# Moving the fading of layer 1's states from VectorE to GpSimd

## The reference

```
cb = einsum('bign,bjgn->bijg', C, B)
y  = einsum('bijg,bijgr,bjgrp->bigrp', cb, lmat * dt, x)
y  = y + einsum('bign,bgrpn->bigrp', C, S) * exp(acum)        # the part from the state
w  = exp(a_last - acum) * dt
S  = exp(a_last) * S + einsum('bjgn,bjgr,bjgrp->bgrpn', B, w, x)   # faded, then added to
```

## Time and profile before

| | us |
|---|---|
| median of 3 runs | 1554.14 |
| range of the runs | 1553.2 to 1556.65 |
| the profiled execution | 1551.42 |
| its span, first to last instruction | 1549.7 |

### The profile page before, as it was taken

How to read it: one execution, slowest core, us unless ns; L and a number is a source line. 1 busy time by engine, 2 the same in 40 slices (tenths; PEclk the granted TensorE clock), 3 DMA queues, 4 the chain that set the end, 5 groups by cost and what they waited for, 6 DMA issues and landing times. The chain is left out here.

```text
span 1549.7 us, 31393 instructions
## 1 busy us (share of the span) xinstructions
PE 1447.2 (93%) x11610; PEld 1195.0 (77%) x11610; DVE 1175.9 (76%) x2595; ACT 822.4 (53%) x1837; POOL 248.7 (16%) x438
## 2 busy tenths in 40 slices
PE   6999999799999979899999999989999999999985
PEld 5979787666788858898888888767787777777754
DVE  4555587856786887968977898986879787587775
ACT  4735353446465544546655765653657364655451
POOL 5010113101231200012111112120003110000012
PEclk8999999999999999999999999999999999999998
DMA  6455455335476542547854764843585664554541
GB/s 190 132 155 148 129 168 151 112 114 171 120 205 191 160 122 71 150 122 182 253 145 121 237 191 140 240 140 94 167 247 143 189 183 144 175 150 150 175 137 61
DMA packets 283778, 243.11 MB, mean 157 GB/s; under 512 B 32856, under 2 KB 251036, under 8 KB 283468
## 3 DMA queue, kind: packets, MB, share of 16 engines
q1 hardware_dynamic: 273708, 208.28, 45.6%
q0 software_dynamic: 9920, 32.84, 7.9%
HBM read 180.40 MB, written 64.97 MB: 158 GB/s over the span
## 5 line engine op out<-in xcount | busy, mean ns | idle before, releaser
L1447 PE MATMUL bank<-h,w 128*128 128x268 f32 (+1 forms) x4752 | 835.3, 330 | 22.5 <-ACT w L857 15.8
L1447 PEld LDWEIGHTS bank<-h,w 128*128 128x128 f32 x4752 | 699.4, 191 | 102.1 <-issue 28.4
L873 DVE TENSOR_TENSOR w<-w_raw,w 128x1024 fp32r<-128x1024 f32 x132 | 160.9, 1219 | 35.5 <-ACT w L857 34.9
L842 PE MATMUL bank<-s_w_out,s_yt_hi 128*128 128x512 f32 (+2 forms) x544 | 169.8, 402 | 3.8 <-DVE s_ys L2532 3.8
L857 ACT ACTIVATE w<-w_raw 128x1024 fp32r<-128x1024 f32 x132 | 138.7, 1051 | 8.1 <-DMA w_raw<-in_ssd_w_in_dram 8.1
L1525 DVE SCALAR_TENSOR_TENSOR conv<-before_conv,cw,conv 128x260 f32<-128x260 f32 (+2 forms) x216 | 125.3, 580 | 4.2
L842 PEld LDWEIGHTS bank<-s_w_out,s_yt_hi 128*128 128x128 f32 (+2 forms) x544 | 97.1, 182 | 30.8 <-issue 4.4
L842 PE MATMUL bank<-g_w_out,g_ot_hi 128*128 128x512 f32 (+2 forms) x288 | 97.0, 426 | 1.6 <-DVE g_ot_lo L2073 1.3
L842 PE MATMUL bank<-s_w_out,s_yt_lo 128*128 128x512 f32 x240 | 95.6, 398 | 0.0
L2616 ACT ACTIVATE s_yt_hi<-bank 128x512 fp32r<-128x512 f32 (+1 forms) x36 | 20.1, 557 | 126.5 <-PE bank L2607 126.4
L2319 ACT ACTIVATE s_decay<-s_decay,t_ac 128x128 f32<-128x128 f32 (+1 forms) x288 | 85.4, 379 | 1.2
(11 more groups left out here) (256 smaller groups left out, 2503.4 us busy)
## 6 DMA issues: line engine op xcount, KB each, us to landing
w_raw<-in_ssd_w_in_dram SPq DMA_DIRECT2D x80, 512.0 KB, 4.3
w_raw<-in_gla_w_in_dram SPq DMA_DIRECT2D x48, 512.0 KB, 4.3
s_decay<-kept_acd SPq DMA_DIRECT2D x32, 512.0 KB, 6.2
w_raw<-in_ssd_w_out_dram SPq DMA_DIRECT2D x30, 512.0 KB, 4.0
g_chunk<-kept_gq SPq DMA_DIRECT2D x32, 448.0 KB, 4.9
s_chunk<-kept_sq SPq DMA_DIRECT2D x32, 384.0 KB, 4.8
kept_sq<-stage SPq DMA_DIRECT2D x80, 134.0 KB, 4.3
kept_sq<-stage SPq DMA_DIRECT2D x40, 256.0 KB, 4.7
```

What stands on the lines that cost most here:

```text
L842: last = pe.matmul(bank[0:r, :], yt[a][:, k, 0:r], wo[:, b, 512 * half:512 * half + 512], start=(k + a + b == 0), stop=(k == tiles - 1 and ...
L873: dve.tensor_tensor(self.part(i, 1), self.raw(i), hi, ALU.subtract).then_inc(self.w_lo, 1)
L1447: last = pe.matmul(bank[:, 0:n], w[:, p.tile % 2, a, k, :], h[:, b, k, c:c + n], start=(i == 0), stop=(i == len(terms) - 1))
```

## The change

GpSimd does the fade of the state, in a new function pool_fade, called at each scan with s > 0 at the scan's place in the list. It waits for the decay (el_done) and for TensorE's read of the old state (inter). VectorE scales the state part first, after a wait for s_prod, then waits for the new semaphore s_faded and adds SU. The semaphore aexped is given up for the new one: the exponential of a_log now counts on exped.

```diff
@@ program, gpsimd
             elif name == "keep":
                 ssd.pool_keep(pool, *at)
+            elif name == "scan" and at[2]:
+                ssd.pool_fade(pool, *at[1:])
@@ Sizes.act_log
         if G == 0:
-            act.activation(self.m["aexp"][:, :], self.m["alog"][:, :], ACT.Exp).then_inc(self.aexped, 1)
+            act.activation(self.m["aexp"][:, :], self.m["alog"][:, :], ACT.Exp).then_inc(self.exped, 1)
         act.wait_ge(self.absd, GROUP_CGS[G][-1] + 1)
         act.activation(t1, t1, ACT.Exp, scale=-1.0).then_inc(self.exped, 1)
-        act.wait_ge(self.exped, G + 1)
+        act.wait_ge(self.exped, G + 2)
@@ Sizes.dve_sum
-        dve.wait_ge(self.aexped, 1)
@@ Ssd.dve_scan
-        dve.wait_ge(self.el_done, e + 1)
         if s:
+            dve.wait_ge(self.el_done, e + 1)
             dve.wait_ge(self.inter, self.z_count(u, s) + 1)
-            kept = self.mark(dve.tensor_tensor(heads(S), heads(S), self.by_head(t["el"][:, e % 2, :], P), ALU.mult))
             dve.wait_ge(self.s_prod, e + 1)
-            dve.wait_ge(self.chain, kept)
+            from_state = self.mark(dve.tensor_tensor(heads(xw[0:n, :]), heads(self.Y[1][0:n, :]),
+                                                     self.by_head(t["ea"][0:n, e % 2, :], n), ALU.mult))
+            dve.wait_ge(self.s_faded, self.z_count(u, s) + 1)
             dve.tensor_tensor(S, S, self.SU[:, :], ALU.add).then_inc(self.s_new, 1)
         if not self.last_unit(u, s):
             skip()
-        if s:
-            from_state = self.mark(dve.tensor_tensor(heads(xw[0:n, :]), heads(self.Y[1][0:n, :]),
-                                                     self.by_head(t["ea"][0:n, e % 2, :], n), ALU.mult))
         dve.wait_ge(self.intra, e + 1)
         dve.wait_ge(self.skipped, e + 1)
@@ Ssd
+    def pool_fade(self, pool, u, s):
+
+        e, q, heads = ev(u, s), self.z_count(u, s), self.split_heads
+        S = self.S[:, u % 2, :]
+        pool.wait_ge(self.el_done, e + 1)
+        pool.wait_ge(self.inter, q + 1)
+        pool.tensor_tensor(heads(S), heads(S), self.by_head(self.t["el"][:, e % 2, :], P),
+                           ALU.mult).then_inc(self.s_faded, 1)
```

More of the change, by code:

```diff
@@ L1174, in __init__ @@
         self.m, self.d = m, d
-        (self.small_in, self.aexped, self.absd, self.exped, self.logged, self.dt_done, self.a_done, self.scanned, self.ea_done, self.stored) = (
-             sem("size_" + x) for x in ("small_in", "aexped", "absd", "exped", "logged", "dt_done",
+        (self.small_in, self.absd, self.exped, self.logged, self.dt_done, self.a_done, self.scanned, self.ea_done, self.stored) = (
+             sem("size_" + x) for x in ("small_in", "absd", "exped", "logged", "dt_done",
                                         "a_done", "scanned", "ea_done", "stored"))
@@ L2174, in __init__ @@
          self.yt_lo, self.out_done, self.added, self.xdc_ready, self.spread, self.answered, self.ss_kept, self.ss_new, self.s_turned, self.s_kept, self.parked, self.s_saved,
-         self.z0_in, self.z0_turned, self.answers_turned) = (
+         self.z0_in, self.z0_turned, self.answers_turned, self.s_faded) = (
              sem("s_" + x) for x in (
@@ L2180, in __init__ @@
                  "xdc_ready", "spread", "answered", "ss_kept", "ss_new", "s_turned",
-                 "s_kept", "parked", "s_saved", "z0_in", "z0_turned", "answers_turned"))
+                 "s_kept", "parked", "s_saved", "z0_in", "z0_turned", "answers_turned", "s_faded"))
     def mark(self, ins):
```

## The result

| | before | changed |
|---|---|---|
| median of the runs, us | 1553.67 | 1573.05 |
| range of 4 runs each, us | 1552.95 to 1556.65 | 1570.38 to 1574.33 |
| the profiled execution, us | 1551.42 | 1573.76 |
| its span, us | 1549.7 | 1572.1 |

The changed kernel is slower: its time is 1.0116 times that of before, with a 95% interval of 1.0101 to 1.0131, some 19 us. The forecast was +8, with a range that ended at 1567. The sign was right, the size was not.

A forecast was written before the change was run, and what follows sets the result against it. TensorE, busy 93%, was taken as the bound, with time lost only where it stands still. Middle part +4.75 and last unit +3.05 gave +7.8 us, 1562 on the median; forecast's own range 1557.6 to 1565.7, whole range 1551 to 1567.

The forecast's parts named there:

- The price of a fade: GpSimd's time per 128x512 fade, estimated from its own additions: 1.31 us, low end 0.69, high end 1.84.
- The five named scans: Scans at 914, 935, 986, 1026 and 1197 us: late fades make TensorE stand 6.6 us more in all.
- A: Time at which the last of GpSimd's tasks ahead of a scan's fade ends; new states forecast by A + 2.1.
- They cost nothing as long as that margin holds.: Some ten other scans with late A: no cost while L2574's margin or VectorE's idle time holds, else up to 0.5 us each.
- The reordering puts the fade beside work that does not hold it up.: At each scan the fade runs beside VectorE work reading a PSUM bank and one SBUF operand, so it is not stretched.
- The take-backs: After the 914 and 1026 us scans, TensorE's lateness shortens later waits for VectorE: 0.55 and 0.6 us taken back.
- -0.7 at the first scan: After the first scan VectorE is 0.69 us earlier, and TensorE's 2.1 us wait for L1514 shrinks by all of it.
- The last unit: Scans at 1506 and 1520 us delay ys by 2.1 and 0.95 us; the two scans before taken as 0: +3.05 us.
- A microsecond of standing as a microsecond of time: TensorE's summed stands, +7.8 us, counted in full as kernel time: 1559.2 on the profiled execution, 1562 on the median.
- VectorE held up by the fade: Rival: at about ten scans L873, L875 or L1525 stand up to 1.31 us for the fade; +11.6, 1565.7; chance 0.13.
- The relief comes through: Rival: five L842 waits on ys save 0.69 us each, plus L1514's; -4.1 us, 1550.0; chance 0.22.
- Hidden: Rival: late scans' stands only replace later VectorE waits, relief cancels the last unit; 0 to +3, 1555.6; chance 0.20.

The follow-up runs named there:

- the fades first: Changed kernel with GpSimd's sample DMA pairs, roots and stores that stood just ahead of a fade moved behind it; 1550.21 us, ratio 0.9962 against the kernel before.

## Why the prediction was right or wrong

**The price of a fade.** Taken as 1.31 us, measured at 1.06: too high by 0.25. That worked toward less loss than forecast, and is no cause of the miss. The estimate of 1.16 worked out from the figure of the Trainium skill (GPSIMD Engine Reference, "Elementwise — side-by-side cycle accounting") was the nearer one. The low end (0.69) and the high end (1.84, for 1.83 in the worst case) held.

**The five named scans.** By how much further TensorE fell behind its counterpart there: 1.0 us at the first (forecast 1.2), 0.7 at the second (0.95), 1.8 at the third (2.1), 0.7 at the fourth (1.0), and 1.3 at the fifth, taken at the products (1.35). Together 5.5 for 6.6. Going through the scans one by one, with A from GpSimd's row, was right.

**"They cost nothing as long as that margin holds."** This step failed. TensorE fell behind by 1.4 us at 907.60, 0.8 at 1139.97 and 0.6 at 1485, where nothing stood in the sum. The margin was read from the kernel before, and the change itself used it up. At 907.60 the transposes had stood none before; now A + 1.05 is when everybody waits. At 1139.97 the transposes don't wait at all: VectorE's addition does, for 1.34 us, the projection's L1515 is queued behind it, and TensorE waits 1.02 us for that (0.18 before, none with the fades first). The prediction had listed what waits for the addition, but not in these scans what VectorE does behind it. The 0.6 at 1485 is the new order and not the late fade: it is 0.6 with the fades first as well.

**"The reordering puts the fade beside work that does not hold it up."** This step failed too, and the sum had no term for it: 1.4 us more at 812.25, the largest of the places without a term, came mostly from VectorE being held up (1.6 us, against the 0.69 that it no longer spends on the fade; with the new order alone the stand there is 1.75 us and not 2.66), with 1.6 us of slower running behind it and 0.8 given back at the next wait. See the rivals below.

**The take-backs.** Forecast -0.55 and -0.6 for waits that TensorE meets later anyway, after the first and the fourth scan: the profiles have -0.4 after each, so this was about right. Of the -0.7 at the first scan 0.3 came. TensorE's wait for L1515 there fell from 2.14 to 1.74 us, as it did with the order alone, and the one for the states by 0.2. A wait for weights of L875 grew by 0.3, where L1526 and L1539 had taken 1.16 and 1.01 us for their usual 0.50 and 0.16 beside the fade.

**The last unit.** Forecast +3.05 from two scans. The products fell behind by 1.75 and 0.6 us at these two (forecast 2.1 and 0.95), and came 0.5 earlier at one of the two scans taken as 0; then the clock, which before had fallen in the scan ahead and here did not, gave some of it back. In the first profile 1.6 us remain; in the second the unit is 0.8 us faster than before.

**A microsecond of standing as a microsecond of time.** This step failed as well, and it has the most of the miss. TensorE's standing grew by 10.3 us from 705 us on (9.5 from the first scan with a fade), for +7.8 in the sum: a miss of some 2. The time grew by 19 (medians) or 22 (profiles). Of the rest, some 6.6 us lie in layer 1 as slower running. Of these, the 1.6 and 1.3 us right behind the stands of 2.66 and 2.11 us belong to the change, since they come back in every profile with a late fade; the others may be chance. Some 5 us lie in layer 0, where no mechanism of the change is known. The prediction had looked at the granted clock in one window only the earlier trace rows and given it no term. The Trainium skill (TensorE: Matmul & The Clock Gate, Part 1) describes a clock that follows how busy TensorE has recently been; the windows of layer 1 agree, and the prediction had not weighed it.

**The rivals.** *VectorE held up by the fade* was given 0.13 and 1565.7. It happened, both ways: seven instructions of VectorE were stretched by 0.4 us or more, by 5.2 us in all, and the fade itself up to 1.83 us. The two kernels with the new order and no fade on GpSimd have none. In the first scan it cost TensorE 0.3 us. At 807 us it cost VectorE 1.6 us. The stand at 812.25 is 2.66 us for 1.75 with the order alone, and the 1.6 us of slower running come only behind the longer one: together some 2.5 us. So it is part of the loss, and not the main part: with the fades first six instructions are stretched too, by 3.7 us, and that kernel is faster than before. *The relief comes through* was given 0.22 with its condition, that the fade is done before the scaling ends. With the fade first this holds in 28 of 32 scans, and that kernel ran at 1550.21, where the rival had said 1550.0; in the changed kernel it holds in 14. The condition was the right one, but that the two times are so close is partly luck: the waits for ys fell from 8.3 to 6.0 us only, where the rival had five times 0.69. *Hidden* is out.

**The causes, as the runs leave them.** Shown: the semaphore edit is nothing; the order of VectorE alone costs about 5 us (0.8 to 7.9); the fade's place behind the sample pair, the root or the store, together with its 1.06 us, makes the rest of layer 1's loss (22.8 us come back when the place is changed, some 5 of them in layer 0; 7.6 are lost when the length is doubled). Shown by all profiles together: about 3 us are clock, behind two stands that the change made longer. Argued only, from single profiles: the other 3 to 4 us of slower running in layer 1, and the share of VectorE's hold-up. Open: the stretch in layer 0.

## What to carry to other kernels

Before work is moved to an engine that seems idle, ask not for its busy share (16% here) but for what stands just ahead of the work in its queue, and move the work ahead of that: the same edit was worth +19 us or -5. A scan that had a margin may have none left once the change has used it up, so each place needs the new time of everything queued behind the late instruction, not only of the one that waits for it. And a stand of TensorE may cost more than its length: here the granted clock fell behind two of them, for 1.6 and 1.3 us more.

## What the runs showed of the hardware

The fade, a GpSimd multiplication of 128x512 by a factor repeated along rows, took 1.03 to 1.06 us undisturbed. That is 1.5 times VectorE's 687 ns, when the small additions had suggested 1.9.

VectorE and GpSimd hold each other up, VectorE by more than any row of before showed. The last unit of the changed kernel (timeline, then all of L877 in ns minimum/median/maximum):

```profile
1509.73 1.03 POOL L2543 TENSOR_TENSOR states<-states,s_e_last 128x512 f32<-128x512 f32 x1
...
1509.91 1.94 DVE L877 SCALAR_TENSOR_TENSOR s_w_out<-w_raw,wn,s_w_out 128x1024 fp32r<-128x1024 f32 x1 [0.25 <-ACT s_w_out L868]
```

```profile
L877 DVE SCALAR_TENSOR_TENSOR s_w_out<-w_raw,wn,s_w_out x30: 1272/1279/1943, 753.4 to 1509.9; 128x1024 fp32r<-128x1024 f32 x30
```

L877 takes 1.28 us in nearly all of its 30 rows and 1.94 here: it started 0.18 us into the fade, and ended 1.09 us after it, 0.19 less than its own length. The same line of the kernel before has 1294 ns at most. The Trainium skill (SBUF — State Buffer, "Who interferes with whom") has this as an exclusive lock between the two; the row agrees, nearly to the full length. It is rare all the same: eight of 32 fades and seven instructions of VectorE were stretched (by 0.1 us or more and by 0.4 us or more), and the second profile of the changed kernel has the same seven lines. None of the seven reads a PSUM bank. The scaling (L2519), which does, took its usual 0.68 to 0.69 us in every row beside a fade.

Three of the seven (L1526 at 756.82, L1529 at 806.33, L1598 at 831.10) should have ended before the row of the fade starts. They stood on while GpSimd was at the sample transfer just ahead of it. In the kernel before, with the same pair of transfers and no fade behind, the copy at 797.73 took 0.20 us. So by these rows VectorE can be held before the fade is seen to start; why, no run shows.
